# Feed-forward of a streaming encoder layer: gate and up projections by seven block products in place of eight, with weight sums and gated activations kept in DRAM

## The reference, cut to what matters

```python
h2 = _rmsnorm(x, g_ffn) * (1 + sc2) + sh2
g = h2 @ f_w_gate                      # (t, 1024) @ (1024, 2816)
u = h2 @ f_w_up
gconv, new_fconv = _causal_dwconv(g, f_conv, f_conv_w, f_conv_b)   # width 3, per channel, along t
x = x + gt2 * ((jax.nn.silu(gconv) * u) @ f_w_down)
...
y = _rmsnorm(x, g_final)
```

## Time and profile before

| | |
|---|---|
| median of the runs | 2941.59 us |
| profiled execution, first to last instruction | 2937.3 us |
| TensorE busy | 2804.8 us |
| VectorE busy | 1340.6 us |
| ScalarE busy | 980.6 us |
| moved by DMA | 355.40 MB, mean 121 GB/s |

### The profile page before, as it was taken

How to read it: one execution, slowest core, us unless ns; L and a number is a source line. 1 busy time by engine, 2 the same in 40 slices (tenths; PEclk the granted TensorE clock), 3 DMA queues, 4 the chain that set the end, 5 groups by cost and what they waited for, 6 DMA issues and landing times.

```text
span 2937.3 us, 42020 instructions
## 1 busy us (share of the span) xinstructions
PE 2804.8 (95%) x16271; PEld 2504.3 (85%) x16271; DVE 1340.6 (46%) x2610; ACT 980.6 (33%) x1700; POOL 255.1 (9%) x412
## 2 busy tenths in 40 slices
PE   4999999999769999997999999999999999999998
PEld 2888889999647777776999998899999888999987
DVE  3533334332366666663433345453333554544447
ACT  2333334332323545453222224322222443222234
POOL 0100000000043333330000000000000000000000
PEclk7999999999769999998999999999999999999999
DMA  9343334121664444435322234532222453322335
GB/s 325 133 145 134 112 117 158 65 74 69 184 215 138 137 137 132 137 102 135 96 60 63 64 96 156 170 108 73 64 64 64 150 172 108 120 74 72 100 131 187
DMA packets 320987, 355.40 MB, mean 121 GB/s; under 512 B 20692, under 2 KB 261990, under 8 KB 320658
## 3 DMA queue, kind: packets, MB, share of 16 engines
q1 hardware_dynamic: 314564, 346.68, 37.1%
q10 hardware_dynamic: 6288, 6.88, 0.8%
...
HBM read 285.63 MB, written 70.10 MB: 121 GB/s over the span
## 4 chain that ended last, share of the span: by engine, by line
PE 51%; DVE 1%; DMA 1%; issue 0%; ACT 0%; SPq 0%; POOL 0%; DVEq 0%; POOLq 0%; ACTq 0%
PE acc_ps L3196 14%; PE acc_ps L3153 12%; PE acc_ps L3152 12%; PE acc_ps L3154 12%; PE acc_ps L3207 1%; DMA f_mid<-in_f_w_down 0%; DMA f_raw<-in_f_w_down 0%; DVE f_h_lo L3462 0%; DVE f_y L3489 0%; DVE f_h_lo L3556 0%; DVE f_xr L3483 0%; DVE f_h_lo L3465 0%; PE acc_ps L3244 0%; DVE f_prod L3477 0%; ACT f_w_hi L3282 0%
## 5 line engine op out<-in xcount | busy, mean ns | idle before, releaser
L3152 PE MATMUL acc_ps<-f_h_hi,f_w_hi 128*128 128x384 f32 (+1 forms) x2112 | 689.1, 326 | 2.9 <-DVE f_w_lo L3406 2.8
L3153 PE MATMUL acc_ps<-f_h_lo,f_w_hi 128*128 128x384 f32 (+1 forms) x2112 | 688.6, 326 | 0.0
L3154 PE MATMUL acc_ps<-f_h_hi,f_w_lo 128*128 128x384 f32 (+1 forms) x2112 | 688.6, 326 | 0.0
L3406 DVE TENSOR_TENSOR f_w_lo<-f_raw,f_w_hi 128x1024 fp32r<-128x1024 f32 x242 | 296.5, 1225 | 647.1 <-ACT f_w_hi L3282 644.6
L3282 ACT ACTIVATE f_w_hi<-f_raw 128x1024 fp32r<-128x1024 f32 x242 | 256.7, 1061 | 799.7 <-PE acc_ps L3154 533.0
L3152 PEld LDWEIGHTS acc_ps<-f_h_hi,f_w_hi 128*128 128x128 f32 x2112 | 397.1, 188 | 3.6 <-DVE f_w_lo L3406 3.0
L3153 PEld LDWEIGHTS acc_ps<-f_h_lo,f_w_hi 128*128 128x128 f32 x2112 | 397.2, 188 | 0.1
L3154 PEld LDWEIGHTS acc_ps<-f_h_hi,f_w_lo 128*128 128x128 f32 x2112 | 397.1, 188 | 0.0
L959 PE MATMUL p_unit<-w_in_hi,p_ht_hi 128*128 128x512 f32 (+1 forms) x544 | 205.0, 377 | 9.8 <-DVE p_ht_lo L698 7.5
L3196 PE MATMUL acc_ps<-f_w_hi,f_mid_hi 128*128 128x512 f32 x660 | 203.5, 389 | 3.0 <-DVE f_mid_lo L3456 3.0
L3196 PE MATMUL acc_ps<-f_w_lo,f_mid_hi 128*128 128x512 f32 x660 | 203.3, 389 | 0.0
...
## 6 DMA issues: line engine op xcount, KB each, us to landing
f_raw<-in_f_w_down SPq DMA_DIRECT2D x120, 512.0 KB, 3.5
f_raw<-in_f_w_gate SPq DMA_DIRECT2D x66, 512.0 KB
f_raw<-in_f_w_up SPq DMA_DIRECT2D x66, 512.0 KB, 3.8
...
```

The source lines that it names most:

```text
L3152: t.matmul(dst, hi, h2_hi[:, k, cols], start=(k == 0), stop=False)
L3153: t.matmul(dst, hi, h2_lo[:, k, cols], start=False, stop=False)
L3154: last = t.matmul(dst, lo, h2_hi[:, k, cols], start=False, stop=(k == KD - 1))
L3406: v.tensor_tensor(w_lo[j][:], raw[j][:], w_hi[j][:], ALU.subtract).then_inc(s_lo[j], 1)
```

## The change

**Gate and up as a 2 x 2 block product.** For one block f the four weight blocks are A11, A12 (gate, first and second half of k) and A21, A22 (up), each 512 x 128; the activations are B11, B12 (first half of k, first and second half of the tokens) and B21, B22. The gate is C11 = A11 B11 + A12 B21 and C12; up is C21 and C22. In place of eight block products there are seven, in Winograd's form of Strassen's algorithm, on sums S1 = A21 + A22, S2 = S1 - A11, S3 = A11 - A21, S4 = A12 - S2 of the weights and T1 = B12 - B11, T2 = B22 - T1, T3 = B22 - B12, T4 = B21 - T2 (the signs are chosen so that P4 adds). Each product is 4 blocks of k times 3 matmuls, 84 matmuls a unit.

**Where the sums come from.** The weight sums of an f are made on VectorE in span 0, split, and stored to DRAM (`store_sums`, 4 x 512 KB); spans 1 and 2 load the high and low parts of S1 to S4 (`load_sums`) and split only A11, A12 and A22. The activation sums of span 0 are made at the start of the feed-forward (`first_low`, `first_high`), those of spans 1 and 2 in four steps k during the first down pass before (`pair_step`, `pair_high`). The buffers of the down weights and of the split `mid` are parts of the weight groups.

**Recombination.** Three PSUM banks a unit, two sets in turn. P1, P6, P7 and P4 add up in one bank; ScalarE copies it after P1 and after P6, and the bank of P5 after P5; VectorE forms C11, C22 and C12 from these copies and the banks. The first tap with the bias goes from VectorE to ScalarE.

**Gated activations.** `mid` has two buffers of one block; each unit's result is stored to DRAM, and each down step loads its 128 x 384 part beside the weights.

**Other.** Four tiles of the mixers and the first loads lie elsewhere in SBUF. The multiplication by taps no longer reads a copy made on VectorE (`copy_tap` on ScalarE).

The diff, cut to its core:

```diff
+PRODUCTS = ((0, W_A11, B11), (1, W_A12, B21), (0, W_S2, T2), (2, W_S1, T1), (0, W_S3, T3), (2, W_S4, B22), (0, W_A22, T4))
+P1, P2, P6, P5, P7, P3, P4 = range(1, 8)
...
+    def store_sums(f):
+        for g in (2, 3):
+            sp.wait_ge(s_lo[g], f + 1)
+            for n, w in enumerate((w_hi, w_lo)):
+                sp.dma_start(sums_at(f, 2 * n + g - 2), group(w, g).bitcast(F32)).then_inc(s_sst[g - 2], 16)
+    def load_sums(s, f, first=False):
+        n = f + s * KF
+        for g, free in ((2, P5), (3, P3)):
+            if first:
+                sp.wait_ge(s_sst[g - 2], 32 * KF)
+                for j in range(2):
+                    sp.wait_ge(s_dused[j], s * NPASS * QF)
+            else:
+                sp.wait_ge(s_prod, n * NP - NP + free)
+            for m, w in enumerate((w_hi, w_lo)):
+                sp.dma_start(group(w, g).bitcast(F32), sums_at(f, 2 * m + g - 2)).then_inc(s_sld[g - 2], 16)
...
+        if not (opening and s == 0):
+            sp.wait_ge(s_mlo, e - 1)
+        if a == 0 and isinstance(f, int) and f < 4:
+            sp.wait_ge(s_mst[j], 16 * (QF * s + QF - 1))
+        elif a == 0 and isinstance(f, int) and f < 6:
+            sp.wait_ge(s_mst[j], 16 * QF * (s + 1))
...
+        sp.dma_start(mid_raw[j][:, 0:w], src).then_inc(s_mraw[j], 16)
...
+    def unit(s, q, j):
+        f = q * 2 + j
+        static = isinstance(f, int)
+        if static and f >= KF - 2:
+            load_dn(s, 0, 0, f - (KF - 2))
+        else:
+            sp.wait_ge(s_lo[4], f + (s * KF + 1))
+            load_raw(s, q + 1, j)
+        if not (static and f == KF - 1):
+            if s == 0:
+                store_sums(f + 1)
+            else:
+                load_sums(s, f + 1)
+        store_mid(s, q, j)
...
+        for order, (b, slot, op) in enumerate(PRODUCTS):
+            which = order + 1
+            if which == P1:
+                pe.wait_ge(s_lo[1], n + 1)
...
+                    pe.wait_ge(s_tlo, 8 * s)
...
+                if not (static and n < 2):
+                    pe.wait_ge(s_mid, n - 1)
...
+            elif which in (P6, P5):
+                if which == P6:
+                    if s:
+                        pe.wait_ge(s_sld[0], n * 32 + (32 - 32 * KF))
+                    else:
+                        pe.wait_ge(s_lo[2], n + 1)
+                    pe.wait_ge(s_p1, n + 1)
...
+            elif which == P7:
+                if s:
+                    pe.wait_ge(s_sld[1], n * 32 + (32 - 32 * KF))
+                else:
+                    pe.wait_ge(s_lo[3], n + 1)
+                pe.wait_ge(s_u2, n + 1)
+            elif which == P3:
+                pe.wait_ge(s_p5, n + 1)
+            else:
+                pe.wait_ge(s_lo[4], n + 1)
+                pe.wait_ge(s_c22, n + 1)
...
+            opening, dst = which in (P1, P2, P5), bank[j][b][:, 0:w]
+            for k in range(4):
+                hi, lo = (x[:, slot * BLK + k * P:slot * BLK + (k + 1) * P] for x in (w_hi, w_lo))
+                t.matmul(dst, hi, h_hi[:, op, k, 0:w], start=(opening and k == 0), stop=False, skip_group_check=True)
+                t.matmul(dst, hi, h_lo[:, op, k, 0:w], start=False, stop=False, skip_group_check=True)
+                last = t.matmul(dst, lo, h_hi[:, op, k, 0:w], start=False, stop=(k == 3), skip_group_check=True)
+            last.then_inc(s_prod, 1)
...
+            act.wait_ge(s_sum, n * 4 + (2 if g == 2 else 4))
...
+            act.wait_ge(s_prod, n * NP - NP + {1: P2, 2: P5, 3: P3, 4: P4}[g])
+            if g in (2, 3):
+                act.wait_ge(s_sst[g - 2], n * 32)
...
+        a_.activation(group(w_hi, g), raw_group(g, j), ACT.Copy).then_inc(s_hi[g], 1)
...
+    def unit(s, q, j):
+        f = q * 2 + j
...
+        A_, _, C_ = bank[j]
+        act.wait_ge(s_prod, n * NP + P1)
...
+            act.wait_ge(s_c11, n)
+        a_.activation(part[:, 0, 0:w], A_[:, 0:w], ACT.Copy).then_inc(s_p1, 1)
+        if final:
+            down_high(s, 0, 0, 0)
...
+        else:
+            high(s, q + j, 1 - j, 1)
+        act.wait_ge(s_prod, n * NP + P6)
...
+            act.wait_ge(s_c12, n)
+        a_.activation(part[:, 1, 0:w], A_[:, 0:w], ACT.Copy).then_inc(s_u2, 1)
...
+        act.wait_ge(s_prod, n * NP + P5)
...
+            act.wait_ge(s_c22, n)
+        a_.activation(part[:, 2, 0:w], C_[:, 0:w], ACT.Copy).then_inc(s_p5, 1)
...
+        if final:
+            down_high(s, 0, 0, 1)
+        elif s == 0:
+            high(s, q + j, 1 - j, 2)
+            high(s, q + j, 1 - j, 3)
+        else:
+            act.wait_ge(s_prod, n * NP + P3)
+        if final:
+            keep_mid(s, 0, 0, 0)
+        act.wait_ge(s_tap, n + 1)
+        act.wait_ge(s_c12, n + 1)
+        prompt = spans[s][1]
+        last = a_.activation(conv[:, 0:prompt], g_buf[:, 0:prompt], ACT.Identity, scale=tap[:, 0:1], bias=tap[:, 3:4])
...
+        last.then_inc(s_tap0, 1)
+        if not final:
+            high(s, q + j, 1 - j, 4)
+        act.wait_ge(s_conv, n + 1)
...
+            act.wait_ge(s_mid, n)
+        width = spans[s][2]
         a_.activation(gate_on[:, 0:width], conv[:, 0:width], ACT.Silu).then_inc(s_on, 1)
-
-    def step(s, f, last=None):
-        split(0, unit(s, f))
-        if last is not None:
-            keep_g(s, last)
-        split(1, unit(s, f))
+        if not final:
+            copy_tap(f + 1)
...
+    def sum_22(n, w, a_bank):
...
+        dve.wait_ge(s_prod, n * NP + P7)
+        dve.wait_ge(s_p5, n + 1)
+        v.tensor_tensor(part[:, 3, 0:w], a_bank[:, 0:w], part[:, 2, 0:w], ALU.add).then_inc(s_c22, 1)
...
+    def unit(s, q, j):
+        f = q * 2 + j
...
+        A_, D_, C_ = bank[j]
         if s:
             own(v.tensor_copy(g_buf[:, 0:2], at_f(tail, f)[:, 16:18]))
...
-        own.settle()
-        dve.wait_ge(s_gk, f + (s * KF + 1))
+        dve.wait_ge(s_prod, n * NP + P2)
+        dve.wait_ge(s_p1, n + 1)
+        v.tensor_tensor(g_buf[:, 2:2 + w], D_[:, 0:w], part[:, 0, 0:w], ALU.add).then_inc(s_c11, 1)
...
+            sum_22(n, w, A_)
+        if s == 0 and not final:
+            add_weights(q + j, 1 - j, 0)
+            add_weights(q + j, 1 - j, 1)
+        if final:
+            down_low(s, 0, 0, 0)
+        else:
+            low(s, q + j, 1 - j, 1)
...
+            sum_22(n, w, A_)
+        if final:
+            down_low(s, 0, 0, 1)
+        elif s == 0:
+            low(s, q + j, 1 - j, 2)
+        dve.wait_ge(s_prod, n * NP + P3)
+        dve.wait_ge(s_u2, n + 1)
+        here = prompt - w
...
+        v.tensor_tensor(g_buf[:, 2 + w:2 + prompt], C_[:, 0:here], part[:, 1, 0:here], ALU.add).then_inc(s_c12, 1)
+        if final:
+            keep_mid_low(s, 0, 0, 0)
+        elif s == 0:
+            low(s, q + j, 1 - j, 3)
...
-        own(v.tensor_scalar(conv[:, 0:n], g_buf[:, 0:n], tap[:, 0:1], tap[:, 3:4], ALU.mult, ALU.add))
...
-        own.settle()
-        own(v.scalar_tensor_tensor(conv[:, 0:n], g_buf[:, 1:n + 1], tap[:, 1:2], conv[:, 0:n],
...
+        dve.wait_ge(s_c12, n + 1)
+        dve.wait_ge(s_tap0, n + 1)
+        own(v.scalar_tensor_tensor(conv[:, 0:prompt], g_buf[:, 1:prompt + 1], tap[:, 1:2], conv[:, 0:prompt],
                                    ALU.mult, ALU.add))
...
-        own(v.tensor_copy(at_f(tail, f)[:, 16:18], g_buf[:, n:n + 2]))
...
+        own(v.tensor_copy(at_f(tail, f)[:, 16:18], g_buf[:, prompt:prompt + 2]))
         own.settle()
...
-        v.scalar_tensor_tensor(conv[:, 0:n], g_buf[:, 2:n + 2], tap[:, 2:3], conv[:, 0:n],
+        v.scalar_tensor_tensor(conv[:, 0:prompt], g_buf[:, 2:prompt + 2], tap[:, 2:3], conv[:, 0:prompt],
                                ALU.mult, ALU.add).then_inc(s_conv, 1)
-
-    def multiply(s, f):
-
-        dve.wait_ge(s_on, f + (s * KF + 1))
-        dve.wait_ge(s_used[1], unit(s, f) + 1)
-        for b, (at, w) in enumerate(spans[s][2]):
-            last = v.tensor_tensor(at_f(mid, f)[:, at:at + w], gate_on[:, at:at + w], u_ps[:, b, 0:w], ALU.mult)
-        last.then_inc(s_mid, 1)
-
-    def step(s, f, last=None):
-        split(0, unit(s, f))
-        if last is not None:
-            convolve(s, last)
-            multiply(s, last)
-        split(1, unit(s, f))
+        if not final:
+            low(s, q + j, 1 - j, 4)
+        dve.wait_ge(s_on, n + 1)
+        dve.wait_ge(s_prod, n * NP + P4)
...
+            dve.wait_ge(s_mst[j], q * 16 + 16 * QF * s)
...
+        v.tensor_tensor(mid[j][:, 0:w], A_[:, 0:w], gate_on[:, 0:w], ALU.mult)
+        v.tensor_tensor(mid[j][:, w:2 * w], part[:, 3, 0:w], gate_on[:, w:2 * w], ALU.mult).then_inc(s_mid, 1)
...
+    def first_low(order, op, src):
...
+        v.tensor_tensor(h_lo[:, op], src, h_hi[:, op], ALU.subtract).then_inc(s_h0lo, 1)
+    b11, b12, b21, b22 = (h_first[:, k:k + 4, at:at + HALF] for k, at in ((0, 0), (0, HALF), (4, 0), (4, HALF)))
+    add_weights(0, 0, 0)
+    first_low(1, B11, b11)
+    low(0, 0, 0, 1)
+    first_low(2, B21, b21)
...
+    v.tensor_tensor(t1_first[:], b12, b11, ALU.subtract).then_inc(s_t0, 1)
...
```

(20 more changed lines are left out.)

673 lines of the change are left out of this document (435 added, 238 removed).

## The result

The changed kernel takes 2911.06 us (median of 4 runs, 2906.75 to 2914.76) beside 2943.43 (2938.99 to 2948.29) for the kernel before: ratio 0.9888, 95% interval 0.9869 to 0.9908. The gain is 32 us; 74 were forecast. The profiled execution took 2913.92 us, span 2912.1.

A forecast was written before the change was run, and what follows sets the result against it. The feed-forward was taken as bound by TensorE's number of matmuls. Span 2937.3 - 129.8 (fewer matmuls) + 6 + 17 + 15 + 9.4 + 3.7 + 5 (stalls) = 2863.6 us; with 4.3 for the runs' median, 2868 us, range 2843 to 2925.

The forecast's parts named there:

- the entry: Start of the feed-forward: TensorE waits for VectorE's first sums and low parts; 15 us, 2.3 of it for half clock.
- rival D: The stalls overlap each other and the clock holds, so half of the 56 us: 2840 us; chance 0.12.
- The width and the order hi, lo, hi inside a product stay, so the rate per matmul stays too: Gate/up matmuls: spacing stays at 172.7 ns in spans 0 and 1 and 146.2 ns in span 2.
- Gate/up to down: Three span changes: down step 2 loads only after the last activations' store, 2.8 us, plus 0.3 at step 1; 9.4 us.
- stores, 5: Down steps where stores of y block SP: 1 us at each of two places, 3 in the last stage; 5 us.
- sums fill gaps: Down steps: sums of the next span's activations, 12.6 of 16.3 us on VectorE, fit into gaps; no time added.
- tile waits: Units 1 to 3 of spans 1 and 2: P1 copy behind the previous span's squares; 2.55 and 3.2 us each, 17 us.
- span 2's others: Steady units of span 2: P6 waits for ScalarE's P1 copy; 0.27 us in each of 22 units, 6 us.
- sums at the span changes: Down to gate/up, twice: unit 0's sums load only after the last down step; 1.5 + 2.2 = 3.7 us.
- rival E: Every product start behind its waits costs 0.15 us, 69 us in all: 2937 us, no change; chance 0.05.
- C: Rival: the transfer queue becomes the bound at 210 GB/s, 142 us more, 3010 us; chance 0.08.
- B: Rival: the chain inside units costs 0.7 us more in each of 66 units, 46 us, 2914 us; chance 0.25.

The follow-up runs named there:

- e12: Kernel before, TensorE held at units 1 to 4 of each span by one 256-byte DRAM-to-DRAM copy each; 2983.58 us, ratio 1.0142.
- e9: Changed kernel with 32 bytes moved ahead of f_h_hi, so f_h_hi and f_h_lo both start at a multiple of 64 bytes; 2901.45 us, ratio 0.9858.
- e2: Changed kernel with the pair loads (next span's activations) issued behind the down weights and their sums one down step later; 2892.02 us, ratio 0.9829.
- e11: Changed kernel with the down weights of steps 2 and 3 loaded ahead of the store of the last gated activations; 2894.54 us, ratio 0.9837.

## Why the prediction was wrong

The stage tells it without the noise ahead of it. The forecast's sum for it is 1560.3 - 129.8 + 56.1 = 1486.6; it took 1530.5. The 43.9 us between:

- **The clock, a term that the sum had only at the entry, 25.5 us.** Each stall was priced at its own length; only the entry got something for half clock, 2.3 us, and rival D even let "the clock hold" to gain. 51.0 us more at 1.2 GHz cost half of that, at most: in 4.4 us of them TensorE stood idle, which takes off 2.2. e12 shows it with only the pauses added: 23.9 us of waits, 39.2 us of stage. The earlier trace rows had shown a start from rest at half clock; I did not carry that over to the stalls that I was adding myself.
- **"The width and the order hi, lo, hi inside a product stay, so the rate per matmul stays too" failed, 8.2 us.** The rate hung on a third thing, where the two activation tiles start; e9 gives 8.8 us back by ratio (0.9888 to 0.9858, hardly clear of the runs' noise) for 32 bytes, and its distance is 173.3 ns again. The distances before were read a little short, too: 172.7 and 146.2 ns come from counts that include matmuls cut by the window's edges; from start to start they are 173.3 and 146.7, and 130.2 us go in place of 129.8.
- **Gate/up to down, 9.4 us, and stores, 5: mis-sized.** Down-pass waits are 27.5 us against 3.0 before. Step 2 was priced at 2.8 us and took 5.08 in span 0, 2.66 and 2.46 in the others. The rest lies inside the down passes, where the prediction had "sums fill gaps" and no term: pair loads ahead of a weight load in SP's queue and beside it on the DMA engines. e2 took away six of those waits (12.9 us), e11 most of step 2's (10.2 us became 1.1).
- **All waits together were near: 61.0 us more than before, 56.1 forecast, 2.3 of it for the clock.** The entry was near: unit 2 began 45.6 us after the first matmul, 16.5 more than two units of 84 x 173.3 ns; before it was 35.8 and 2.6, so the entry cost 14 us, 15 forecast. The down passes took 10 more. The pattern inside was right: tile waits of 2.54, 2.54, 2.45 and 3.48, 3.48, 3.52 us for 2.55 and about 3.5, span 2's others 0.33 each for 0.27, sums at the span changes 2.31 and 3.06 for 1.5 and 2.2, no table load beside the Silus, TensorE without a wait in spans 0 and 1 beyond the units named, VectorE busy 192 of 250 us in span 0, the 77% forecast.
- **The 5.3 us left are mostly late starts behind the waits.** The prediction gave TensorE 0.1 us to get going again (0.15 in rival E), with no row for it. In the traces the first matmul behind a wait and the one after it start 0.25 us later, together, than the idle time accounts for: below, 0.69 us lie between two starts, where the matmul's own distance is 0.15 and the idle time 0.37, since that is counted from the matmul's end, 0.31 us after its start; and the next start is late by 0.07 more.
```profile
2608.61 0.31 PE L3326 MATMUL acc_ps<-f_h_hi,f_w_lo 128*128 128x320 f32 x1
2609.30 0.38 PE L3324 MATMUL acc_ps<-f_h_hi,f_w_hi 128*128 128x320 f32 x1 [0.37 <-ACT f_part L3464]
2609.52 0.31 PE L3325 MATMUL acc_ps<-f_h_lo,f_w_hi 128*128 128x320 f32 x1
```
  Over the 45 waits inside the stage that is 11.2 us, against 0.8 for 3 before. The shorter distance in span 2 (2.6 us) and the idle time counted twice under the clock (2.2) take part of it back, with smaller terms. So a steady unit of span 2 took 12.76 us, 0.44 above 84 x 146.7 ns, where 0.27 was forecast: 10 us in 22 units in place of 6.

Of the rivals, C did not come (past unit 4 of a span one unit waits for DMA, 0.53 us at 2545.43), nor E (in the steady units only P6 of span 2 starts behind a gap). B's number, 2914, is almost the result, but by luck and not by its cause: span 0's chain had no wait. The Trainium skill (TensorE: Matmul & The Clock Gate, "Wait - 56ns, not 53.3ns?") counts 2.5 ns beyond the columns; here it was 13.3 or 15.5, by the place of the tiles.

The Trainium skill (the same page, "HAM oscillation - how this bites in real kernels") has a matmul kernel in which the wait for each tile's DMA sends TensorE back to the slow clock. The traces here agree with that for 7 of e12's 12 pauses. The prediction cited the page for its matmul rate and passed over this part, which spoke against the change.
